# Gated delta net in a hybrid decoder layer: norms of q and k in channel rows, first half of the block inverse made one pair earlier, transposes of the inverse by VectorE

## The reference: what is computed

```python
q_g = l2norm(cq) * GDN_SCALE          # after conv and SiLU; l2norm(x) = x * rsqrt(sum(x*x) + 1e-6) over 128 channels
k_g = l2norm(ck)
# per chunk of 64 tokens, per v head; g_ = log decay, b_ = beta
gam = cumsum(g_)
L = exp(where(incl, gam[:, None] - gam[None, :], -inf))
A = where(strict, (k_ * b_) @ k_.T * L, 0)
X = triangular_solve(A + eye, [v_ * b_, k_ * b_ * exp(gam)])
v_new = u - w @ S                      # u, w = the two halves of X
attn = (q_ @ k_.T) * L
o = (q_ * exp(gam)) @ S + attn @ v_new
S = exp(g_last) * S + (k_ * exp(g_last - gam)).T @ v_new
```

## Time and profile before

| | us |
|---|---|
| median of 3 runs | 3809.09 |
| range of the runs | 3806.0 to 3810.84 |
| the profiled execution: time | 3810.7 |
| the profiled execution: span, first to last instruction | 3808.6 |
| PE busy in the span | 3618.6 (95%) |
| DVE busy | 2215.3 (58%) |
| ACT busy | 1804.1 (47%) |
| POOL busy | 887.1 (23%) |

### The profile page before, as it was taken

The page is one execution under the profiler, slowest core; times in us unless marked ns, Lnnn a source line. Parts: engine busy times, 40 slices in busy tenths (PEclk is TensorE's granted clock), DMA queues, the critical chain, the costliest instruction groups (busy, mean ns, idle before and its releaser), DMA issues.

```text
span 3808.6 us, 78902 instructions
## 1 busy us (share of the span) xinstructions
PE 3618.6 (95%) x25051; PEld 3300.9 (87%) x25051; DVE 2215.3 (58%) x4379; ACT 1804.1 (47%) x3850; POOL 887.1 (23%) x1051
## 2 busy tenths in 40 slices
PE   8999999999999999999999999999895999999997
PEld 2699999998889889988899888897784999999996
DVE  2566666647665565656565656546667555555555
ACT  1345445455544444455454544455463444444443
POOL 2122222201245444440344544411100000000000
PEclk9999999999999999999999999999996999999998
DMA  8645445568733334438543333357882555555553
GB/s 280 205 136 144 140 139 149 143 180 272 210 99 98 98 101 112 119 95 255 161 126 105 97 101 96 98 160 241 262 248 87 163 165 162 166 160 167 162 165 108
DMA packets 887592, 587.96 MB, mean 154 GB/s; under 512 B 23602, under 2 KB 820244, under 8 KB 886932
## 3 DMA queue, kind: packets, MB, share of 16 engines
q1 hardware_dynamic: 861268, 510.50, 46.8%
q0 software_dynamic: 26240, 76.41, 6.5%
HBM read 545.83 MB, written 40.99 MB: 154 GB/s over the span
## 4 chain that ended last, share of the span: by engine, by line
PE 80%; DVE 7%; issue 5%; ACT 3%; DMA 3%; POOL 1%; DVEq 0%; SPq 0%; ACTq 0%; POOLq 0%
PE acc L575 20%; PE acc L577 19%; PE acc L576 19%; PE acc L547 3%; PE bank L785 2%; PE bank L771 2%; PE bank L805 2%; PE bank L820 1%; DMA raw<-in_w_ada 1%; ACT whi L988 1%; DVE wlo L1462 1%; PE bank L587 1%; DVE h_S L1617 1%; PE bank L769 1%; PE bank L588 1%
## 5 line engine op out<-in xcount | busy, mean ns | idle before, releaser
L1462 DVE TENSOR_TENSOR wlo<-raw,whi 128x512 fp32r<-128x512 f32 x1799 | 1283.3, 732 | 954.9 <-ACT whi L988 936.8
L988 ACT ACTIVATE whi<-raw 128x512 fp32r<-128x512 f32 x1799 | 1097.9, 628 | 933.6 <-PE acc L577 881.3
L575 PE MATMUL acc<-ahi,whi 128*128 128x288 f32 x4112 | 1311.5, 319 | 28.9 <-DVE alo L1959 16.2
L576 PE MATMUL acc<-alo,whi 128*128 128x288 f32 x4112 | 1239.3, 301 | 0.0
L577 PE MATMUL acc<-ahi,wlo 128*128 128x288 f32 x4112 | 1234.8, 300 | 0.0
L575 PEld LDWEIGHTS acc<-ahi,whi 128*128 128x128 f32 x4112 | 797.0, 194 | 52.9 <-issue 32.6
L576 PEld LDWEIGHTS acc<-alo,whi 128*128 128x128 f32 x4112 | 798.9, 194 | 13.2 <-issue 11.5
L577 PEld LDWEIGHTS acc<-ahi,wlo 128*128 128x128 f32 x4112 | 798.9, 194 | 0.0
L575 PE MATMUL acc<-ohi,whi 128*128 128x288 f32 x1792 | 536.4, 299 | 6.1 <-DVE wlo L1462 3.4
L576 PE MATMUL acc<-olo,whi 128*128 128x288 f32 x1792 | 531.3, 296 | 0.0
L577 PE MATMUL acc<-ohi,wlo 128*128 128x288 f32 x1792 | 529.6, 296 | 0.0
(11 more groups left out here) (431 smaller groups left out, 4586.2 us busy)
## 6 DMA issues: line engine op xcount, KB each, us to landing
raw<-in_w_in SPq DMA_DIRECT2D x386, 512.0 KB, 4.1
raw<-in_w_ada SPq DMA_DIRECT2D x192, 512.0 KB, 4.7
raw<-in_w_up SPq DMA_DIRECT2D x128, 512.0 KB, 4.1
raw<-in_w_down SPq DMA_DIRECT2D x128, 512.0 KB, 3.8
raw<-in_w_out_gdn SPq DMA_DIRECT2D x64, 512.0 KB, 5.0
raw<-in_w_o SPq DMA_DIRECT2D x34, 512.0 KB, 4.8
raw<-in_w_out_hg SPq DMA_DIRECT2D x32, 512.0 KB, 5.4
g_S<-in_state_gdn POOLq DMA_DIRECT2D x32, 512.0 KB, 6.0
```

The source lines that it names most:

```text
L575: mm(bank[:, 0:T], whi[:, s, r, :], hi[:, kt, :], start=(kt == 0), stop=False, skip_group_check=True)
L576: mm(bank[:, 0:T], whi[:, s, r, :], lo[:, kt, :], start=False, stop=False, skip_group_check=True)
L988: f(whi[:, s], raw[:, r], ACT.Copy).then_inc(sg["hi_made"], 1)
L1462: tt_(wlo[:, s], raw[:, r], whi[:, s].bitcast(F32), SUB).then_inc(sg["lo_made"], 1)
```

## The change

Of the work on a pair, this moves from the body behind it (`delta_second`, `delta_prev`, `prev`) into its own body (`delta_first`, `delta_own`, `own`): decay matrices, k.k and q.k, A, masks, level 0. In parts:

- **Norms.** ScalarE squares q (s = 14) and k (s = 22) in channel rows, TensorE multiplies with ones (s = 16, 24) so that every row holds the sum, ScalarE takes ln and exp (s = 17, 25), VectorE scales g_C in place (s = 19, 27). The six squares in token rows, g_tq, the six transposes at s = 0 and the copies g_qT, g_kT are gone.
- **Decay matrices and k.k** at s = 31 and s = 30 of the own body, k.k and q.k together in two multiplications of 256 columns. The exponentials follow at s = 32, and VectorE makes A and the masked q.k at s = 33.
- **Level 0**: VectorE masks k.k (g_Ui), makes g_T = ident - beta L k.k from it at s = 35 with a new table column (-beta exp(g)), and transposes it within blocks of 32x32 (`flip`, STREAM_TRANSPOSE). The transposes of level 0 by TensorE and GpSimd's level 0 and g_T are gone.
- **Levels 2 to 5**: g_T is a transposition of g_Ui by VectorE behind each subtraction, in place of four transposes by TensorE and a copy.
- **Places.** Everything of `delta_second` from s = 6 on moves 4 steps forward (UT 1 to s = 6, the 8-column multiplications to s = 9, g_uTs to s = 12, the output to s = 37, its norm to s = 40). The list of conv steps is unchanged.
- **GpSimd**: `decay_rows(n+1)` stands ahead of the load of the next states; levels 1 and 2 and g_at are made in `own(n+1)`, ahead of the scaled copies of k.

```diff
-        PU, UT = (8, 12, 15, 18, 21), (10, 14, 17, 20, 23)
-        WS, DS = (30, 34, 38), (28, 32, 36, 40)
+        PU, UT = (4, 8, 11, 14, 17), (6, 10, 13, 16, 19)
+        WS, DS = (26, 30, 34), (24, 28, 32, 36)
...
+                if s in (16, 24):
+                    k = (s - 16) // 8
+                    pe.wait_ge(sg["g_nsq"], EARLIER + 2 * j + k + 1)
+                    pe.wait_ge(sg["g_qn"], EARLIER + 2 * j + k)
...
+                    mm(R[7][:, 0:T], ones[:, :], gns[:, 0, :], start=True, stop=True).then_inc(sg["g_nss"], 1)
+                if s == 30:
+                    pe.wait_ge(sg["g_qn"], EARLIER + 2 * j + 2)
+                    pe.wait_ge(sg["g_snew"], 2 * j)
+                    for a in range(2):
+                        mm(R[7][:, 2 * a * P:2 * (a + 1) * P], gC[:, 1, a * P:(a + 1) * P], gC[:, 0:2, a * P:(a + 1) * P], start=True, stop=True)
+                    mm(R[4][0:NS, 0:2 * NS], gC[:, 1, TP:T], gC[:, 0:2, TP:T], start=True, stop=True).then_inc(sg["g_kk"], 1)
+                if s == 31:
+                    pe.wait_ge(sg["g_gr"], EARLIER + j + 1)
...
-                if s == 0:
-                    pe.wait_ge(sg["g_tokqk"], EARLIER + n + 1)
-                    pe.wait_ge(sg["g_ors"], n)
-                    for bank, src in ((R[7], gtq), (R[4], gtk)):
-                        for a in range(3):
-                            last = turn(bank[:, a * P:(a + 1) * P], src[:, a], ident[:, :])
-                    last.then_inc(sg["g_qk_turned"], 1)
...
-                        for p in range(4):
-                            turn(R[6][:, p * P:(p + 1) * P], gUi[:, p, :], ident[:, :])
...
-                if s == 16:
+                if s == 12:
                     pe.wait_ge(sg["g_vt"], EARLIER + n + 1)
...
+                if s == 32:
+                    act.wait_ge(sg["g_d"], EARLIER + j + 1)
+                    for a in range(2):
+                        f(gGR[:, a].rearrange("p k e s -> p (k e s)"), R[2 + a][:, :], ACT.Exp)
+                    f(gGRs[:, :].rearrange("p k e s -> p (k e s)"), R[4][0:NS, 384:512], ACT.Exp).then_inc(sg["g_ex"], 1)
...
+                if s == 35:
...
+                            stt(gT[:, 2 * a + e, :], gUi[:, a, :], gsf[:, e, 6 + a:7 + a], ident[:, :], MUL, ADD)
...
+                    flip(gUi[:, :, :].rearrange("p q s -> p (q s)"), gT[:, :, :].rearrange("p q s -> p (q s)"))
...
-                    copy(gT[:, :, :], R[6][:, :].rearrange("p (q s) -> p q s", s=P)).then_inc(sg["g_tnew"], 1)
...
+                    if l < 5:
+                        dve.wait_ge(sg["g_unew"], 5 * n + l)
+                        flip(gT[:, :, :].rearrange("p q s -> p (q s)"), gUi[:, :, :].rearrange("p q s -> p (q s)")).then_inc(sg["g_tnew"], 1)
-                if s == 15:
+                if s == 11:
                     dve.wait_ge(sg["g_qws"], n + 1)
```

More of the change, by code:

```diff
@@ L289, in hybrid_layer @@
             gvn = gqp
-            gqT = sb("g_qT", [P, T])
-            gkT = sb("g_kT", [P, T])
+            gns = sb("g_ns", [P, 2, T])
             gqpT = sb("g_qpT", [P, 2, TP])
@@ L708, in delta_first @@
-                    last.then_inc(sg["g_turned"], 1)
+                    pe.wait_ge(sg["g_qn"], EARLIER + 2 * j + 2)
+                    pe.wait_ge(sg["g_ex"], EARLIER + j + 1)
+                    pe.wait_ge(sg["g_qkm"], EARLIER + j + 1)
+                    pe.wait_ge(sg["g_vn"], 4 * j)
+                    pe.wait_ge(sg["g_st"], 4 * j)
+                    for k in range(4):
+                        for a in range(3):
+                            m = P if a < 2 else NS
+                            bank, col = token_place(k, a)
+                            last = turn(bank[0:m, col:col + P], gC[:, k, a * P:a * P + m], ident[:, :])
@@ L1375, in _ @@
             ts, tt_, stt, rec = nc.vector.tensor_scalar, nc.vector.tensor_tensor, nc.vector.scalar_tensor_tensor, nc.vector.reciprocal
-            copy = nc.vector.tensor_copy
+            copy, flip = nc.vector.tensor_copy, nc.vector.transpose
             MUL, ADD, SUB = ALU.mult, ALU.add, ALU.subtract
@@ new lines, in delta_own @@
+                if s == 35:
+                    dve.wait_ge(sg["g_y"], EARLIER + j + 1)
+                    dve.wait_ge(sg["g_ut"], 5 * j)
+                    for a in range(2):
+                        for e in range(2):
+                            stt(gT[:, 2 * a + e, :], gUi[:, a, :], gsf[:, e, 6 + a:7 + a], ident[:, :], MUL, ADD)
+                    for e in range(2):
+                        last = stt(gTs[:, e, :], gUs[0:NS, 0, :], gsf[0:NS, e, 8:9], ident[0:NS, 0:NS], MUL, ADD)
+                    last.then_inc(sg["g_t1"], 1)
+                    dve.wait_ge(sg["g_t1"], j + 1)
+                    flip(gUi[:, :, :].rearrange("p q s -> p (q s)"), gT[:, :, :].rearrange("p q s -> p (q s)"))
+                    flip(gUs[0:NS, :, :].rearrange("p e s -> p (e s)"), gTs[:, :, :].rearrange("p e s -> p (e s)")).then_inc(sg["g_u1"], 1)
@@ L2206, in load_delta, with decay_rows @@
                     pool.dma_start(gS0[:, e], pair_of(state_gdn, j)[e]).then_inc(sg["g_s0"], 16)
-            def own(j):
-                pool.wait_ge(sg["g_sc"], EARLIER + j + 1)
+            def decay_rows(j):
+                pool.wait_ge(sg["g_sf"], EARLIER + j + 1)
                 pool.wait_ge(sg["g_attn"], j)
@@ L2219, in own @@
                 last.then_inc(sg["g_gr"], 1)
+            def own(j):
+                level(j, 1)
+                level(j, 2)
+                pool.wait_ge(sg["g_qkm"], EARLIER + j + 1)
+                pool.wait_ge(sg["g_o"], j)
+                for a in range(2):
+                    pt(gat[:, a], gGR[:, a, 1], gQKm[:, a, :].unsqueeze(1).to_broadcast([P, 2, P]), MUL)
+                pt(gats[0:NS, :, :], gGRs[:, 1], gQKms[:, :].unsqueeze(1).to_broadcast([NS, 2, NS]), MUL).then_inc(sg["g_attn"], 1)
+                pool.wait_ge(sg["g_sc"], EARLIER + j + 1)
                 pool.wait_ge(sg["g_tokqk"], EARLIER + j + 1)
-                pool.wait_ge(sg["g_o"], j)
                 pool.wait_ge(sg["g_ds"], 4 * j)
```

292 lines of the change are left out of this document (128 added, 164 removed).

## The result

| | kernel before | changed kernel |
|---|---|---|
| median, us | 3809.15 (4 runs, 3806.0 to 3810.84) | 3838.72 (4 runs, 3829.66 to 3847.19) |
| span of the profiled execution, us | 3808.6 | 3828.1 |
| ratio, with 95% interval | 1 | 1.0078 (1.0052 to 1.0104) |

What follows compares the result with a forecast made beforehand. TensorE, busy 95% of the span, was taken as the bound. Work 2.3, waits 0.5 and clock 0.5 gave 3.3 us a pair, 53 over 16; with the ends, taken as 60: 3749 us, range 3700 to 3795.

Steps and rivals of the forecast that it cites:

- The work term: TensorE, every pair: transposes and other work removed, less the added norms, save 2.3 us a pair, 37 us over 16.
- The old waits: TensorE's waits for g_QW and GpSimd's level 0: 26 of 28 us in seven pairs go, 3.7 us a pair.
- The three new waits: TensorE waits at s = 12, 31 and 40: 1.4, 0.1 and 1.6 us a pair.
- the walk: The new order followed through one body with measured rows: new waits of 3.5 us a pair against 4.0 now.
- R3: Rival: VectorE falls behind at s = 33 to 38, waits 4.8, 2.1 and 1.5 us, 64 us slower, 3873; chance 0.10.
- the output's norm, s = 40: TensorE reaches s = 40 at 13.1 us, the VectorE and ScalarE chain ends at 14.7: wait 1.6 us a pair.
- R2: Rival: new waits as long as the old, 4 to 4.5 us, clock unchanged, 3775; chance 0.20 shared with another rival.
- Wait 1: TensorE at s = 12 waits for VectorE's g_uTs: 1.6 us at full clock, taken as 1.4 a pair.
- Wait 2: TensorE at s = 31 waits for GpSimd's decay rows: 0.1 us a pair, 1 if VectorE is late.
- small waits: TensorE's small waits for subtractions: 0.4 us a pair.
- the clock term: Half-clock time behind TensorE's waits: 0.5 of 1.4 us a pair given back, bounds -0.7 and 1.4.
- the last pair and the first body: Last pair, beside the gates, gains 4 us more; the first body has no pair behind and nothing late.

Runs made afterwards that it cites:

- GpSimd late: Changed kernel with GpSimd's levels 1 and 2 and g_at held until VectorE's addition g_o for the pair in front: 3751.72 us, ratio 0.9861 to the kernel before.
- both factors: Changed kernel with both parts of the fourth convolution's g_C taking their second factor from PSUM instead of SBUF: 3769.38 us, ratio 0.9891 to the kernel before.
- small dose: Changed kernel with GpSimd waiting for the addition g_o only after its level 1, ahead of level 2: 3776.53 us, ratio 0.9914 to the kernel before.
- one factor: Changed kernel with only the 128x256 part of the fourth convolution's g_C taking its second factor from PSUM: 3823.65 us, ratio 1.0048 to the kernel before.
- g_uTs early, whi ahead of the SiLU: Changed kernel with g_uTs ahead of the convolution of s = 10 and whi of s = 12 ahead of its SiLU: 3805.73 us, ratio 0.999 to the kernel before.

## Why the prediction failed

**What held.** TensorE's instructions fell by the 480 foretold. The work term stood up: 25 of 28 us for its largest part; the rest of it (the norms, the other ten transposes, k.k and q.k) was not run by itself. The old waits for g_QW and for GpSimd's level 0 are gone. The three new waits stand where the walk put them. STREAM_TRANSPOSE takes 0.712 us against 0.69 taken and "0.5 to 0.7" looked for; the estimate of 0.53 us, worked out from the rate in the Trainium skill, "Vector Engine (DVE) Microarchitecture Reference", section 3.8, is not borne out. And the point from which R3 would decide, 6.3 us of new waits a pair, was well placed: 73.5 + 33.6 + 10.1 = 117.2 us in 16 pairs are 7.3, and the kernel is slower.

**The step that failed** is the third of the walk, "the output's norm, s = 40". It added VectorE's instructions, each with the duration that it has when nothing runs beside it: "a chunk 0.5, wlo 0.6, g_C 0.5". For wlo has a row; for g_C it has none, though 0.5 was a fair reading of the kernel before (0.42 at most). In the trace after, wlo is 1.58 and g_C 3.12, and the wait is 4.6 us a pair for 1.6. With GpSimd out of the way the same wait is 17.3 / 16 = 1.1. The walk never asked what GpSimd does in these microseconds, although the change itself puts its levels 1 and 2 and the masks there, released by the transposition L1761 shortly ahead of g_C. R2 had "where GpSimd's level 1 and 2 now run beside the next ones" in a clause, without a price. R3 had nearly the measured sizes of the two large waits (4.8 and 2.1 us; its 1.5 for the third was 0.7) but from a slow transposition, which is not slow.

**The clue was in the trace of before**, but not in the rows of g_C. The prediction set GpSimd aside with the engines that are busy under 60% of the time. VectorE and GpSimd of the kernel before, where GpSimd made its levels 0 and 1 and g_T:

```profile
1049.79 1.48 DVE L1462 TENSOR_TENSOR wlo<-raw,whi 128x512 fp32r<-128x512 f32 x1
1051.20 3.33 DVE L1765 TENSOR_TENSOR g_z<-g_ca,g_ce 128x288 f32<-128x288 f32 x1
1054.45 0.24 DVE L1703 COPY g_U<-bank 128x96 f32<-128x96 f32 x1
```

```profile
1049.45 1.28 POOL L2243 TENSOR_TENSOR g_lev<-g_A,levm 128x512 f32<-128x512 f32 x1 [2.77 <-DVE g_As L1776]
1050.68 0.77 POOL L2245 TENSOR_TENSOR g_levs<-g_As,levm 32x64 f32<-32x64 f32 x1
1051.42 1.26 POOL L2243 TENSOR_TENSOR g_lev<-g_A,levm 128x512 f32<-128x512 f32 x1
1052.65 0.32 POOL L2245 TENSOR_TENSOR g_levs<-g_As,levm 32x64 f32<-32x64 f32 x1
1052.94 1.27 POOL L2253 TENSOR_TENSOR g_T<-ident,g_lev 128x512 f32<-128x512 f32 x1
```

The same hold was there already: wlo takes 1.48 us, and 3.33 the product g_z, which like g_C has both factors in SBUF and takes 0.43 at its shortest. With these 0.8 and 2.9 us more in the third step, the walk would have given 1.6 + 3.7 = 5.3 us for this wait; the mean was 4.6, the longest 4.9.

This is what the Trainium skill says in "SBUF — State Buffer", section "Who interferes with whom": VectorE and GpSimd share a pair of ports under an exclusive lock, which a VectorE instruction with two SBUF inputs needs against a GpSimd instruction that reads SBUF, and one with at most one SBUF input, outside the two-port modes, does not. The runs agree on who is held: 3.12 us with both factors in SBUF, 0.41 with one in PSUM, at the same place beside the same GpSimd work. On how long they differ: the page gives the lock for one whole instruction, while g_C was held over three of GpSimd's, level 2 and the two masks g_at. The page would have spoken against this change, and I had not weighed it.

**The other waits.** Wait 1 came out at 2.2 us for 1.4. In the stretch shown for g_uTs the three later instructions of the convolution take 2.61 us where GpSimd works beside them, and 1.7 elsewhere: 0.9 us, which would cover the 0.8. That is read off the trace, not tried by itself. Wait 2 was 0.7 for 0.1; copying g_sf four steps earlier took it away.

**The clock.** The forecast gave back 0.5 us a pair for it. In the runs each us of the wait for g_n that was taken away brought more than itself. By the spans of the profiled executions: 77 us for 56.2 (GpSimd late), 72 for 49.2 (g_C behind g_o), 58 for 42.7 (both factors), 53 for 40.8 (small dose), 8 for 6.9 (one factor): 1.2 to 1.5. For the waits at the start of the body (g_uTs early, whi ahead of the SiLU) it is 16 us for 17.7, so there nothing more came; why is not shown. With that measure the new waits explain the miss: 3.0, 0.8 and 0.6 us a pair over the forecast are 70 us, less the 6 of small waits that did not come, is 64, and 64 x 1.2 to 1.5 = 77 to 96. The profiled execution missed the forecast in its own terms (3751) by 79, the median by 90. The sum of the forecast set the new waits against the old ones and hardly priced what a long wait costs in clock behind it.

**Partly luck:** the 3752 us with GpSimd late and the forecast of 3749 agree in the total, less so in the terms. The period fell by 4.4 us a pair in the seven pairs (83.7 to 79.3), more than the 3.3 of the sum, at a clock of 0.97 where 0.95 to 0.96 was looked for. So the sum was too small for a pair, the clock term above all. Outside the pairs it was too large. The forecast added 7 us there, for the last pair and the first body. Measured, the first 8-column multiplication comes 1.5 us later (1068.2 for 1066.7), and from the last one (2466.8 before, 2404.2 here) to the end of the span it is 1346.7 us for 1341.8: 6 us lost in place of 7 gained. What makes that end longer is open.

## What to carry to other kernels

When a change moves work of one engine beside another's, price each instruction on the critical row under the work that will then run beside it, and look in the trace of before for instructions of the same kind at their longest, not only for the same one at its usual duration: g_C was never long there, g_z was. On VectorE, ask where each operand lies: beside GpSimd, products with both factors in SBUF and a copy from SBUF to SBUF were held here, and what had a factor in PSUM was not, so order the ones that can be held behind the result that is waited for. And when a wait is removed, follow the chain through the other engine's queue (here convolution, SiLU, whi, wlo, subtraction) before counting it as gained.

## What the runs showed of the hardware

- A hold of VectorE can outlast one instruction of GpSimd: g_C, begun at 2110.59, ended at 2113.7, and between these GpSimd ran level 2 and both masks g_at back to back; a product of 32 columns was held for 2.56 us in the same way.
- GpSimd is held too: its 32x64 product takes 0.77 us where VectorE's wlo is in between and 0.32 elsewhere.
- VectorE's transposition is not held. Between SBUF tiles, 128x512 of 4 bytes, its mean is 712 ns; 17 of the 64 for g_T in the changed kernel lie wholly beside GpSimd's work, and they take 0.71 us too.
